# Two transformer blocks in one kernel: half of the index copies issued by ScalarE's queue, key copies, latent squares and latent norms moved later, and index scores begun sooner

## The reference, cut to what matters

```python
h = rmsnorm_2(x, norm_g)
(q_lat, c_kv, k_rope, z_a, q_b, k_b, v_b, z_b,
 q_idx, k_idx, w_idx, gate_a, gate_b) = split(h @ w_in, cuts)
# MLA: low-rank latents, normed, then spread to 8 heads
q  = (rmsnorm_2(q_lat, g_q_lat) @ w_uq)      # 384 -> 8 x (64 + 32)
kv = (rmsnorm_2(c_kv, g_kv_lat) @ w_ukv)     # 256 -> 8 x (64 + 64)
# q's last 32 and k_rope (shared by all heads) are rotated by position
y_a = softmax(q k^T, chunk-causal) v
# DSA: an index picks 128 keys for each query
s     = q_idx . k_idx   (8 heads of 32)
score = sum over heads of relu(s) * w_idx    # top_k(score, 128)
y_b = softmax over the picked keys of (q_b k_b^T + rel_bias) v_b
x = x + (sigmoid(gate_a) * (y_a @ w_o_a) + sigmoid(gate_b) * (y_b @ w_o_b)) @ w_out
```

## Time and profile before

| what | value |
|---|---|
| median of 3 runs (lowest, highest) | 1103.9 us (1103.29, 1106.97) |
| the profiled execution | 1105.54 us |
| its span, first to last instruction | 1103.7 us |
| PE busy | 1056.7 us, 96% of the span |
| DVE, ACT, POOL busy | 612.5, 461.1, 252.2 us |
| mean granted clock of PE | 0.983 |
| DMA moved | 102.32 MB, mean 93 GB/s |

### The profile page before, as it was taken

One profiled execution on the slowest core, in us unless ns is written; L12 is line 12 of the kernel. 1 busy time (PEld: TensorE's weight loads), 2 busy tenths in 40 slices (PEclk: granted clock), 3 DMA queues, 4 the chain that ended last, 5 costly groups with the idle time before them and its releaser, 6 DMA issues.

```text
span 1103.7 us, 13481 instructions
## 1 busy us (share of the span) xinstructions
PE 1056.7 (96%) x5152; PEld 849.2 (77%) x5160; DVE 612.5 (55%) x1049; ACT 461.1 (42%) x808; POOL 252.2 (23%) x155
## 2 busy tenths in 40 slices
PE   7989999999999999999999998899999999999996
PEld 6868787677888888888888776777887766788885
DVE  6584367757444433454445466898756664425544
ACT  6426345545323221222234465555755444423322
POOL 1362332222111100001014333322322322321100
PEclk9998899999999999999999999999999998999998
DMA  8111142212332232222332426211213323122322
GB/s 288 62 58 59 39 117 83 73 58 77 103 108 94 98 115 96 77 96 96 99 112 77 127 61 211 77 58 58 91 61 99 91 92 103 59 95 96 99 74 77
DMA packets 34799, 102.32 MB, mean 93 GB/s; under 512 B 4560, under 2 KB 8032, under 8 KB 34736
## 3 DMA queue, kind: packets, MB, share of 16 engines
q1 hardware_dynamic: 34736, 101.47, 28.1%
HBM read 93.35 MB, written 4.74 MB: 89 GB/s over the span
## 4 chain that ended last, share of the span: by engine, by line
PE 73%; DVE 14%; ACT 6%; issue 4%; SPq 2%; DMA 1%; POOL 1%; DVEq 0%; ACTq 0%; POOLq 0%
PE bank L1373 20%; PE bank L1377 20%; PE bank L1375 20%; PE bank L1507 2%; PE bank L1498 2%; DVE m L2073 1%; DVE score L2075 1%; PE bank L1387 1%; DVE score L2064 1%; PE bank L1388 1%; PE bank L1389 1%; ACT WH L1559 1%; PE bank L1479 1%; DVE small L1957 1%; DVE f_s L1861 1%
## 5 line engine op out<-in xcount | busy, mean ns | idle before, releaser
L1373 PE MATMUL bank<-HH,WH 128*128 128x512 f32 x808 | 330.0, 408 | 7.8 <-ACT HH L1567 5.9
L1377 PE MATMUL bank<-HH,WL 128*128 128x512 f32 x808 | 318.5, 394 | 0.0
L1375 PE MATMUL bank<-HL,WH 128*128 128x512 f32 x808 | 318.4, 394 | 0.0
L2156 POOL TENSOR_TENSOR WL<-WS,WH 128x1024 fp32r<-128x1024 f32 x64 | 154.9, 2420 | 367.8 <-ACT WH L1559 367.2
L1373 PEld LDWEIGHTS bank<-HH,WH 128*128 128x128 f32 x808 | 154.5, 191 | 43.7 <-ACT WH L1563 5.8
L1559 ACT ACTIVATE WH<-WS 128x1024 fp32r<-128x1024 f32 x161 | 167.8, 1049 | 41.9 <-PE bank L1377 41.0
L1377 PEld LDWEIGHTS bank<-HH,WL 128*128 128x128 f32 x808 | 153.6, 190 | 33.6
L1375 PEld LDWEIGHTS bank<-HL,WH 128*128 128x128 f32 x808 | 154.1, 191 | 29.4 <-issue 0.5
L1810 DVE TENSOR_TENSOR WL<-WS,WH 128x1024 fp32r<-128x1024 f32 x97 | 126.4, 1310 | 34.2 <-ACT WH L1559 34.1
L2204 POOL TENSOR_TENSOR fa<-fa,fg 128x512 f32<-128x512 f32 x22 | 28.3, 1286 | 273.4 <-DVE fa L2010 273.4
L1373 PE MATMUL bank<-GH,WH 128*128 128x512 f32 x176 | 68.5, 389 | 0.0
(11 more groups left out here) (335 smaller groups left out, 1736.2 us busy)
## 6 DMA issues: line engine op xcount, KB each, us to landing
WS<-wall SPq DMA_DIRECT2D x161, 512.0 KB, 3.4
scratch<-rows SPq DMA_DIRECT2D x8, 320.0 KB, 5.3
X<-xT SPq DMA_DIRECT2D x8, 256.0 KB, 6.5
b_t<-scratch SPq DMA_DIRECT2D x8, 256.0 KB, 3.8
outT<-X SPq DMA_DIRECT2D x8, 256.0 KB, 2.1
b_m<-b_m SPq DMA_DIRECT2D x11, 128.0 KB, 4.3
f_s<-f_s SPq DMA_DIRECT2D x8, 128.0 KB
f_m<-f_m SPq DMA_DIRECT2D x8, 128.0 KB
```

Source lines behind the costliest of these rows:

```text
L1373: e.matmul(b[:, :], wh, xh[:, at_k, :], start=k == 0, stop=False)
L1375: e.matmul(b[:, :], wh, xl[:, at_k, :], start=False, stop=False)
L1377: m = e.matmul(b[:, :], wl, xh[:, at_k, :], start=False, stop=k == n - 1)
L2156: e.tensor_tensor(WL[:, u % NW, :], WS[:, u % NST, :], f32(WH[:, u % NW, :]), ALU.subtract).then_inc(*tick(w_low_g, u))
```

## The change

- `lat_out` emits only the latent's scaling at the end of its product. Square, halves and release of tmp are kept in a list and emitted after the first pair of the next product (`with_squares`).
- The key latent's sums and `norm_kv` move from behind ql0 into the z product, directly ahead of the query latent's sum and `norm_q`. `norm_kv` now holds only its two logarithms, and `norm_q` the logarithm of the query norm and then all three exponentials.
- The twelve copies of index_stack j = 1 are issued on ACT's queue, right after ACT's own i_qh copy of that step; those of j = 0 stay on SP.
- The key copies are a step of their own, `send_keys`, behind the z product.
- For p = 0, mla_products takes mla_v's blocks in between its products: block 0, uk0, block 1, uq0, block 2, uq1, block 3. The weight unit of the value blocks counts as used when block 3 is done.
- Six side steps go ahead of the first score in place of nine, and the rate is 1.1 side steps for each score in place of 1.0.

```diff
             def out(b):
                 m, t, free = tmp_ring.take()
                 do("latent", c=c, x=x, name=name, b=b, t=t, free=free)
-                add_square((x, c), total_g, t[:, :], None, out_v(name))
-                do("halve_latent", c=c, x=x, t=t, name=name)
-                tmp_ring.give(m, low((x, c)))
-                known.add((x, c))
+
+                def rest():
+                    add_square((x, c), total_g, t[:, :], None, out_v(name))
+                    do("halve_latent", c=c, x=x, t=t, name=name)
+                    tmp_ring.give(m, low((x, c)))
+                    known.add((x, c))
+                squares.append(rest)
                 return out_v(name)
             return out
+        squares = []
+
+        def with_squares(gen):
+
+            for n, _ in enumerate(gen):
+                if n == 0 and squares:
+                    squares.pop(0)()
+                yield n
+
         def latents():
             for c in range(2):
-                yield from product(f"ckv{c}", "w_in_2", 0, cols(P_CKV + 128 * c), "h3", NK,
-                                   lat_out(c, "lk", f"ckv{c}", acc[1]))
+                yield from with_squares(product(f"ckv{c}", "w_in_2", 0, cols(P_CKV + 128 * c), "h3", NK,
+                                                lat_out(c, "lk", f"ckv{c}", acc[1])))
             bias_rows()
             do("row_out")
             for c in range(3):
-                yield from product(f"ql{c}", "w_in_2", 0, cols(P_QL + 128 * c), "h3", NK,
-                                   lat_out(c, "lq", f"ql{c}", acc[0]))
+                yield from with_squares(product(f"ql{c}", "w_in_2", 0, cols(P_QL + 128 * c), "h3", NK,
+                                                lat_out(c, "lq", f"ql{c}", acc[0])))
                 do("copy_rows", heads=((0, 1, 2), (3, 4, 5), (6, 7))[c])
-                if c == 0:
+            for n in with_squares(z_products("za", P_ZA, 0)):
+                if n == 2:
                     i1, b1 = column_sums("lk", acc[1], total_g(("lk", 1)))
                     i2, b2 = token_sums("lkt", [acc[1]], total_g(("lk", 1)))
                     do("norm_kv", b1=b1, b2=b2)
                     t_ring.give(i1, norm_a("lk ln"))
                     t_ring.give(i2, norm_a("lkt ln"))
-            for n, _ in enumerate(z_products("za", P_ZA, 0)):
-                if n == 2:
                     i, b = column_sums("lq", acc[0], total_g(("lq", 2)))
                     do("norm_q", b=b)
                     t_ring.give(i, norm_a("lq ln"))
                 yield
+            do("send_keys")
...
-                    tile(("w_ukv_2", k, column[128:]))
+                    unit_end[tile(("w_ukv_2", k, column[128:])) // UT] = ("av", 3)
...
+            between = mla_v() if p == 0 else iter(())
+            if p == 0:
+                yield next(between)
             yield from product(f"uk{p}", "w_ukv_2", 0, cols(256 * p, 64) + cols(256 * p + 128, 64), "lk", 2, k_out)
             for hl in range(2):
                 hd = 2 * p + hl
+                if p == 0:
+                    yield next(between)
                 yield from product(f"uq{hd}", "w_uq_2", 0, cols(96 * hd, 96) + cols(96 * hd + 80, 16)
                                    + cols(96 * hd + 64, 16), "lq", 3, q_out(hd, hl))
+            yield from between
...
-        side = chain(latents(), mla_v(), mla_products(0))
-        for _ in range(9):
+        side = chain(latents(), mla_products(0))
+        for _ in range(6):
             next(side)
...
-        weave(index_scores(), side, 1.0)
+        weave(index_scores(), side, 1.1)
...
-                elif kind == "index_stack":
-                    j = s["j"]
+                elif kind == "index_stack" and s["j"] == 0:
+                    j = 0
...
-                elif kind == "keys":
+                elif kind == "send_keys":
...
                     e.activation(i_qh[:, j, :], i_q[:, j, :], ACT.Copy).then_inc(*istack_a.tick(("q", j)))
+                    for h in range(4 if j else 0):
+                        r, dst = slice(32 * h, 32 * h + 32), i_qq[4 * j + h]
+                        q.wait_ge(istack_a(("q", j)))
+                        e.dma_start(f32(dst[0:32, 128:T]), f32(i_qh[r, j, 128:T])).then_inc(*index_in[j].tick())
+                        e.dma_start(f32(dst[64:96, 128:T]), f32(i_qh[r, j, 128:T])).then_inc(*index_in[j].tick())
+                    for h in range(4 if j else 0):
+                        r, dst = slice(32 * h, 32 * h + 32), i_qq[4 * j + h]
+                        q.wait_ge(istack_v(("q", j)))
+                        e.dma_start(f32(dst[32:64, 128:T]), f32(i_ql[r, j, 128:T])).then_inc(*index_in[j].tick())
...
-                    q.wait_ge(norm_a("lk ln"))
-                    e.activation(RK[:, :], RK[:, :], ACT.Exp, scale=-0.5).then_inc(*norm_a.tick("lk"))
-                    q.wait_ge(norm_a("lkt ln"))
-                    e.activation(rtok[:, 4:8], rtok[:, 4:8], ACT.Exp, scale=-0.5).then_inc(*norm_a.tick("lkt"))
                 elif kind == "norm_q":
                     q.wait_ge(sums("lq"))
                     e.activation(RQ[:, :], s["b"][:, :], ACT.Ln, scale=1.0 / 384, bias=eps[:, :]).then_inc(
                         *norm_a.tick("lq ln"))
+                    q.wait_ge(norm_a("lkt ln"))
+                    e.activation(rtok[:, 4:8], rtok[:, 4:8], ACT.Exp, scale=-0.5).then_inc(*norm_a.tick("lkt"))
+                    q.wait_ge(norm_a("lk ln"))
+                    e.activation(RK[:, :], RK[:, :], ACT.Exp, scale=-0.5).then_inc(*norm_a.tick("lk"))
```

## The result

| | before | after |
|---|---|---|
| median of 20 runs each (lowest, highest) | 1103.2 us (1100.53, 1106.97) | 1107.1 us (1102.81, 1110.27) |
| ratio to before, 95% interval | | 1.0035 (1.0025 to 1.0045) |
| the profiled execution; its span | 1105.54; 1103.7 us | 1107.32; 1105.5 us |
| mean granted clock of PE | 0.983 | 0.982 |

What follows compares the result with a forecast made beforehand. PE, busy 96% of the span, was taken as the bound, with 11.7 us of waits and slow clock to recover; 6.3 us new or left gave a gain of 5.4, 1103.9 to 1098.5 us, range 1094 to 1105.5.

Steps and rivals of the forecast that it cites:

- the third waits about 0.2 us: Three sums in a row on two banks: the third waits about 0.2 us for the first's logarithm.
- product ended by 679 to 682, DVE behind it by up to 1 us: Last query latent: product end and DVE's lag, from which the query sum's input is ready at about 685.
- 5.50 us: DVE's idling for ACT's i_t until 672.80; bringing the norms together was to remove it.
- nothing: Key copies moved behind the z product: no cost to the weight load behind them; up to 5.7 us without cover.
- rival C: SP and ACT take turns issuing copies; first score waits 9.2 us, 1105.5 us in all; chance 0.20.
- near 654: When SP's first weight load leaves, 13.3 us sooner, with twelve index copies and the key copies off its queue.
- with 1.6 us to spare: ACT's copies delay the weight split for the first query-latent product; PE comes near 660, so it costs zero.
- Scores sooner: First score waits about 2.2 us for its index copies; PE's clock falls behind it, costing 2.9 us.
- rival B: DVE becomes the bound; 3 us return as waits at the query sum or for a_q, 1101.5 us; chance 0.17.
- about 685: When the query sum's input should be ready, so that its 4.4 us wait goes.
- a_q, value blocks: MLA products between value blocks: the 3.0 us of a_q waits shrink to 1.0 us.
- Behind 720 us the gain should be kept.: After 720 us the work order is unchanged and PE nearly full, so the 5.4 us gain should be kept.

Runs made afterwards that it cites:

- two by two: Kernel before with norms together alone, key copies late alone, and both: ratios 1.0024, 0.9990 and 0.9951.
- ladder: Runs one edit at a time, from the kernel before with key copies late and norms together (1098.78 us) to the changed kernel (1107.08 us).
- repaired kernel: Changed kernel with nine side steps, rate 1.0, copies j = 1 on SP and key sums two product pairs earlier: 1099.41 us, ratio 0.9955.
- last kernel: Kernel before with key copies late, norms together, key sums earlier, squares a product later and one early ACT table load: 1097.30 us, ratio 0.9945.
- part 3: The section of repair runs: the repaired kernel, 1099.41 us, and single edits, among them copies j = 1 on ACT again, 1101.41 us.

## Why the prediction was wrong, point by point

The waits that it wanted gone went. What failed is the term **"the third waits about 0.2 us"**, which measured 3.08, and under it the step "product ended by 679 to 682, DVE behind it by up to 1 us": the product ended at 681.12, as forecast, but DVE took it 4.5 us behind. The forecast put its sums on the end of DVE's one long idle piece and did not price what DVE still had in its queue ahead of this latent. Beside it stand terms put at too little: 2.8 us for a_q, a_k and zb in place of 1.0, 3.4 us of clock in place of 2.9, and the 1.2 us at 777 and 0.4 more for Pc in place of nothing. None of its three signs of being wrong came (a first score waiting over 5 us, ql0 waiting for its weights, the wait for acc surviving), so the signs did not cover the step that failed.

- **The bound, and why DVE was late.** The forecast named both causes of the 5.50 us, table loads and the weight unit that SP asked for late, but then gave all of it to the norms and to the key copies "nothing". The two by two shows them as covers of each other: neither alone is worth anything, both are worth 5.4 us. Since the change had both, this cause of the idling was removed; its share was wrong.
- **Copies.** Right in size: 12 issues from 646.9 to 654.6, SP's pitch 0.63 to 0.80, so rival C is refuted. SP's first weight load left at 658.30, not "near 654": its copies were issued by 654.2, but a load also waits for a low half, and ACT, busy with its own copies, split the high half for that only from 654.68. The Trainium skill (Perfetto Trace Analysis, section "DMA Instruction — HWDGE (DVE, Sync)") has the issuing engines share one descriptor generator, locked for exclusive use; here SP's issues took 0.59 to 0.76 us beside ACT's 0.60 to 0.62, so the trace doesn't bear out a price of that size. **Wrong in the price**: the forecast had zero "with 1.6 us to spare", from the cover of the early scores. With the scores late the copies on ACT cost 3.2 us by the ladder, and PE's wait for the weight split is 1.6 us, as the forecast said it would be without the cover. It did not see the latent half, for which DVE idles 7.00 us, longer than the 5.50 that went; no run shows a price for that. With the scores early, the copies' place made no difference.
- **Scores sooner.** The wait was forecast at 2.2 us and came as 2.5, the clock fell, and cost 1.7 instead of 2.9. The forecast gave no term to the rate of 1.1. By the ratios it is worth 2.4 of the 3.6 us that the early scores cost (1.0035 against 1.0013, and against 1.0002). How, stays open: the stretch shows 1.1, and neither the top rounds nor the scores ahead of the last latent can carry it (two rounds in both, 13 scores at rate 1.1 and 14 at 1.0). What the early start does can be read: it puts one top round more ahead of the last latent, and that latent's product ends 36.7 us into the stretch in place of 34.0, behind the wait and the slow clock. DVE's lag behind it shrank by 3.0 us and the product came 2.7 later, so the norms' gain was used up. That is rival B in kind, DVE as the bound: from 665 to 685 us it is busy 18.8 of 20 us, 11.9 before. But the kernel with the scores late has 18.8 as well and takes 1103.57, so a full DVE does not by itself give the changed kernel's time. Early scores in the repaired kernel and rate 1.1 with nine steps were not tried.
- **Norms together.** "The third waits about 0.2 us" measured 3.08. The logarithm that frees the bank stands behind the last latent's square and half, and a table load, on ACT (688.38, 689.67). I had the second sum's length against the logarithm's, not the place of the logarithm in ACT's list. Both inputs of the third sum hang on the late latent: acc (688.40 in place of "about 685") and, through ACT's list, the bank. The clock fell behind this wait too. With the sums two pairs earlier the wait was still 2.2 to 3.5 us, since the logarithm still stood behind the last latent's square; only in the last kernel, with the table load out of the way and the squares late, the bank comes as early as acc.
- **a_q, value blocks.** 1.0 us forecast, 0.2 measured, and 1.9 for a_k beside it: a wait renamed. The ratios give the interleaving nothing; its stretch is 2.4 us shorter in the one pair of profiles, which the times do not bear out.
- **"Behind 720 us the gain should be kept."** The lead at the first waits of the attention is not kept one for one: 1.2 us stand at 777. When I took that one away, Pc waited instead.

The sum had 11.7 us to give back and 6.3 to pay. The 11.7 were given back. What it had to pay was 2.5 us at the first score, 3.1 at the third sum, 2.8 for a_q, a_k and zb, 3.4 of clock, 0.4 more for Pc and 1.2 at 777, 13.4 in all: 1.7 us on the wrong side by the counts, 1.3 in the stretch, 3.9 in the medians. The part of the 3.9 us that is not in the stretch is not explained. And the best of the change was hidden in it: key copies late and norms together, its sums set two pairs earlier, are 5.4 us faster alone.

## What to carry to other kernels

When an engine idles for a result, list everything that would have kept it idle until then, and remove all or none: two overlapping causes each price at zero, and a profile names only the last. When a step moves onto another engine's queue, ask for every consumer of what then stands behind it there; when a product is to be used soon, ask what its reader still has in its queue, not only when the product ends; and when a sum moves, find the place of the instruction that frees its bank, with the table load ahead of it. Try the parts of a change in all combinations when they meet on one engine: here the whole was slower, and two of its six parts, with the key sums two product pairs earlier than the change has them, made a faster kernel.

## What was unexpected of the hardware

The length of a gap does not settle whether the clock falls. At the third sum the repaired kernel has a gap of 2.18 us and keeps 1.00, and the one with the copies on ACT again has 2.19 us and is granted 0.66 in the 5 us around it (the windows in part 3). Near 920 us the changed kernel and the one with rate 1.0 have the same gap, 2.36 and 2.34 us. The windows behind it, first of the changed kernel, then of the other:

```profile
920.00:925.00 5.00, 2.64 (x11) 1.98 (x10) 2.00 (x7) 2.00 (x4) 2.44 (x1) 0.83 0.52 124
925.00:930.00 5.00, 5.00 (x24) 4.08 (x24) 1.04 (x5) 1.01 (x4) 0.00 (x0) 0.82 0.49 157
```

```profile
920.00:925.00 5.00, 4.59 (x27) 3.96 (x28) 1.41 (x8) 0.99 (x3) 1.65 (x1) 1.00 0.42 156
925.00:930.00 5.00, 5.00 (x27) 3.08 (x27) 1.82 (x7) 3.37 (x7) 0.07 (x1) 1.00 0.01 5
```

That gap cost 5 x 0.17 + 5 x 0.18 = 1.75 us of clock in one and nothing in the other. From the wait for sq_late on, where all kernels do the same, the profiled executions took between 213.3 and 218.0 us (216.9 in the changed kernel, 213.4 with rate 1.0, 218.0 in the repaired one). A single profile therefore carries some 4 us that are not the change's, more than what the change is worth; that these are all clock was not shown.
